# Two gathers a slot, one from each expert table, in place of one from the joined table

## The reference

```python
PEER_HEADS, PEER_TOPK, D_MODEL = 8, 16, 1024          # 128 experts a token
...
def peer_ffn(xn, w_query, sub_keys, expert_u, expert_v):   # tables: (16384, 1024) a layer
    ...
    idx = i1 * PEER_N_KEYS + i2
    g = jax.nn.softmax(cv, axis=-1)
    def block(args):
        xb, ib, gb = args
        hid = jax.nn.gelu(jnp.einsum('td,thkd->thk', xb, expert_u[ib]).astype(jnp.float32), approximate=False)
        return jnp.einsum('thk,thkd->td', (gb * hid).astype(xb.dtype), expert_v[ib])
...
for l in range(DEPTH):
    ...
    x = x + merged.astype(x.dtype) @ w_out[l]
    x = x + peer_ffn(rms_norm(x, norm2_w[l]), w_query[l], sub_keys[l], expert_u[l], expert_v[l])
```

## Time and profile before

| | |
|---|---|
| timed runs, median of 3 | 4050.73 us |
| span of the profiled execution | 5878.7 us |
| mean granted TensorE clock in it | 0.555 |
| PE, DVE, ACT, POOL busy | 97%, 49%, 28%, 22% |
| moved by DMA | 1444.45 MB, mean 246 GB/s |
| gathers | 1024 of 1 MB, 1237.6 us busy on POOL |
| the last stage | about 5000 to 5879 us |

### The profile page before, as it was taken

How to read it: one execution, slowest core, us unless ns; L and a number is a source line. 1 busy time by engine, 2 the same in 40 slices (tenths; PEclk the granted TensorE clock), 3 DMA queues, 4 the chain that set the end, 5 groups by cost and what they waited for, 6 DMA issues and landing times.

```text
span 5878.7 us, 40315 instructions
## 1 busy us (share of the span) xinstructions
PE 5726.4 (97%) x13374; PEld 2787.7 (47%) x13374; DVE 2887.4 (49%) x5745; ACT 1648.5 (28%) x4216; POOL 1285.3 (22%) x1094
## 2 busy tenths in 40 slices
PE   9999999999999998999999999899999999899999
PEld 5555555444444545444445545344445555222222
DVE  3321003665555455756555555756555554744443
ACT  3431101344422211244432211245422211222222
POOL 0000000222222221322222221322222221334343
PEclk6555555555555555555555555555555555555555
DMA  4222222767777775767777775777777775899997
GB/s 155 93 102 81 73 90 95 267 238 266 261 275 268 274 280 202 285 245 280 273 272 297 283 291 190 280 256 271 271 268 308 281 290 191 315 350 342 345 342 281
DMA packets 212948, 1444.45 MB, mean 246 GB/s; under 512 B 27256, under 2 KB 27256, under 8 KB 46340
## 3 DMA queue, kind: packets, MB, share of 16 engines
q0 software_dynamic: 164976, 1133.94, 52.0%
q1 hardware_dynamic: 47632, 307.80, 14.4%
q10 hardware_dynamic: 132, 0.12, 0.0%
HBM read 1439.31 MB, written 7.13 MB: 246 GB/s over the span
## 4 chain that ended last, share of the span: by engine, by line
PE 96%; DVE 2%; ACT 1%; issue 1%; DMA 0%; SPq 0%; ACTq 0%; DVEq 0%
PE banks L609 52%; PE sums L871 21%; PE banks L871 7%; PE banks L748 5%; PE banks L827 3%; PE banks L669 2%; PE banks L736 1%; PE banks L786 1%; PE banks L778 1%; PE banks L694 1%; PE banks L844 1%; DVE x L1479 1%; DVE rows L1470 0%; PE banks L637 0%; PE banks L700 0%
## 5 line engine op out<-in xcount | busy, mean ns | idle before, releaser
L609 PE MATMUL banks<-hT,ring 128*128 128x256 f32 x6656 | 2608.4, 583 | 4.7 <-DVE arena L1316 3.9
L609 PEld LDWEIGHTS banks<-hT,ring 128*128 128x128 f32 x6656 | 1507.5, 228 | 1151.7 <-issue 734.0
L576 POOL DMA_INDIRECT rows<-in_w_uv,idx x1024 | 1237.6, 1209 | 3600.3 <-PE sums L871 1981.3
L1470 DVE CUSTOM_DVE_ANT_0 rows<-rows,xn 128x1024 f32<-128x1024 f32 x1024 | 1241.6, 1220 | 530.8 <-DMA rows<-in_w_uv,idx 528.0
L871 PE MATMUL sums<-rows,diag 128*128 128x512 f32 x1612 | 1285.2, 970 | 70.0 <-ACT diag L1076 47.9
L1479 DVE SCALAR_TENSOR_TENSOR x<-rows,wgt,x 128x1024 f32<-128x1024 f32 x493 | 632.0, 1282 | 234.8 <-ACT wgt L1068 234.0
L871 PEld LDWEIGHTS sums<-rows,diag 128*128 128x128 f32 x1612 | 369.2, 232 | 791.7 <-issue 683.2
L1281 DVE SCALAR_TENSOR_TENSOR arena<-banks,pr,arena 128x254 f32<-128x254 f32 (+1 forms) x512 | 246.8, 482 | 354.6 <-ACT arena L965 340.9
L1063 ACT ACTIVATE gelu<-hid 128x2 f32<-128x2 f32 x512 | 102.9, 201 | 1100.7 <-DVE hid L1470 1099.3
L609 PE MATMUL banks<-yT,ring 128*128 128x256 f32 x1024 | 400.2, 582 | 0.0
L871 PE MATMUL banks<-rows,diag 128*128 128x512 f32 x512 | 393.7, 966 | 0.0
(11 more groups left out here) (205 smaller groups left out, 2955.8 us busy)
## 6 DMA issues: line engine op xcount, KB each, us to landing
ring<-in_w_ssd SPq DMA_DIRECT2D x96, 1024.0 KB, 5.4
ring<-in_w_att SPq DMA_DIRECT2D x64, 1024.0 KB, 6.1
ring<-in_w_mrg SPq DMA_DIRECT2D x52, 1024.0 KB, 8.4
arena<-a_rows POOLq DMA_DIRECT2D x32, 1024.0 KB, 7.6
ring<-in_w_qry SPq DMA_DIRECT2D x32, 1024.0 KB, 4.8
arena<-bias_tiles POOLq DMA_DIRECT2D x16, 1152.0 KB, 7.3
ring<-in_w_out SPq DMA_DIRECT2D x16, 1024.0 KB, 7.0
rows<-in_w_uv,idx POOLq DMA_INDIRECT x1024, 6.8
```

Source lines behind the costliest of these rows:

```text
L576: nc.gpsimd.indirect_dma_start(out=rows[n % NB][:, :], out_offset=None, in_=w_uv, in_offset=bass.IndirectOffsetOnAxis(ap=idx[:, t, s:s + 1 ...
L609: mm = pe.matmul(out, w[:, k * P:(k + 1) * P], rhs[:, k0 + k, :], start=start and k == 0, stop=stop and k == n - 1)
L1470: v.tensor_tensor_reduce(u, u, xn2[:, (n // SLOTS_T) % 3, :], 1.0, 0.0, ALU.mult, ALU.add, hid[:, k:k + 1]).then_inc(u_done, 1)
```

## The change

The joined table goes; `w_u` and `w_v` are two inputs. The eight buffers of 8 KB become sixteen of 4 KB: a ring of eight for u rows and a ring of eight for v rows, in the same room. Each slot has two gathers of 128 rows of 4 KB. On POOL, tick n issues the v gather of slot n + 4, when slot n - 4 is summed, and then the u gather of slot n + 7, when the dot product of slot n - 1 is done. The wait for `i_ok` goes with the u gather. DVE waits for the u row's landing before the dot product; PE and DVE wait for the v row's landing before the sum. Lines shift by up to 21 (L1470 becomes L1490, L871 becomes L891, L1479 becomes L1500; L576 stays).

```diff
--- before.py
+++ after.py
@@ -77,7 +77,8 @@
 
 NB = 8
 LAG = 3
-AHEAD = NB - LAG - 1
+AHEAD_V = NB - LAG - 1
+AHEAD_U = NB - 1
 DIAGS = 5
 
 BEHIND = 3.0
@@ -245,7 +246,7 @@
             tick(*todo.pop(0)[:2])
 
 
-def build(nc, x_prompt, x_sample, consts, biases, rel, par, w_ssd, w_att, w_mrg, w_out, w_qry, w_uv,
+def build(nc, x_prompt, x_sample, consts, biases, rel, par, w_ssd, w_att, w_mrg, w_out, w_qry, w_u, w_v,
           w_n2, w_final, y_prompt, y_sample):
     with ExitStack() as ctx:
         def sb(name, shape, dt=F32):
@@ -291,7 +292,9 @@
         gelu = sb("gelu", [P, SLOTS_P])
         wgt = sb("wgt", [P, SLOTS_P])
         diag = [sb(f"diag{n}", [P, P]) for n in range(DIAGS)]
-        rows = [sb(f"rows{n}", [P, 2 * D]) for n in range(NB)]
+        rows_all = sb("rows", [P, 2 * NB * D])
+        rows_u = [rows_all[:, n * D:(n + 1) * D] for n in range(NB)]
+        rows_v = [rows_all[:, (NB + n) * D:(NB + n + 1) * D] for n in range(NB)]
         late_keys = sb("late_keys", [P, 4 * SLOTS_T])
         iota16 = sb("iota16", [P, 16], BF16)
         ident = cst[:, C_ID:C_ID + P]
@@ -327,7 +330,7 @@
         junk = cut(D)
         n2b = cut(D)
         after_n = used[0]
-        first = rows[NB - 1]
+        first = rows_all[:, 2 * (NB - 1) * D:2 * NB * D]
         rel_w, hot_rel, mask_rel, row_rel = first[:, 3 * RW:3 * RW + NG * 8], first[:, 0:RW], first[:, RW:2 * RW], first[:, 2 * RW:3 * RW]
 
         used[0] = 0
@@ -447,7 +450,8 @@
         q_ev, q_s, q_sv = count("q_ev", 16), count("q_s", PH), count("q_sv", PH)
         k_v, i_ok, s_d, s_e, s_v2 = (sem(n) for n in ("k_v", "i_ok", "s_d", "s_e", "s_v2"))
         xn_ok = count("xn_ok", 2)
-        g_in = [sem(f"g_in{n}") for n in range(NB)]
+        u_in = [sem(f"u_in{n}") for n in range(NB)]
+        v_in = [sem(f"v_in{n}") for n in range(NB)]
         u_done, g_ge, g_w, d_ok, v_pe, v_dve = (sem(n) for n in ("u_done", "g_ge", "g_w", "d_ok", "v_pe", "v_dve"))
         x_add = count("x_add", 2)
         f_w, f_ss, f_v, f_sq, f_ok = (sem(n) for n in ("f_w", "f_ss", "f_v", "f_sq", "f_ok"))
@@ -564,27 +568,42 @@
                 pool.wait_ge(x_mid.sem, x_mid.at(m, 2))
                 pool.dma_start(n2b, w_n2[m // 2].partition_broadcast(P)).then_inc(n2_in.sem, 16)
 
-            def gather(n):
+            def gather(n, table, dst, landed):
 
                 p, k = n // SLOTS_P, n % SLOTS_P
                 t = 2 * (p % 2) + k // SLOTS_T
                 s = k % SLOTS_T
+                nc.gpsimd.indirect_dma_start(
+                    out=dst, out_offset=None, in_=table,
+                    in_offset=bass.IndirectOffsetOnAxis(ap=idx[:, t, s:s + 1], axis=0)).then_inc(landed, 16)
+
+            def gather_u(n):
+
+                p, k = n // SLOTS_P, n % SLOTS_P
                 if k == 0 or part_of(p, k) != part_of(p, k - 1):
                     pool.wait_ge(i_ok, part_of(p, k) + 1)
                 if n >= NB:
+                    pool.wait_ge(u_done, n - NB + 1)
+                gather(n, w_u, rows_u[n % NB], u_in[n % NB])
+
+            def gather_v(n):
+
+                if n >= NB:
                     summed(pool, n - NB)
-                nc.gpsimd.indirect_dma_start(
-                    out=rows[n % NB][:, :], out_offset=None, in_=w_uv,
-                    in_offset=bass.IndirectOffsetOnAxis(ap=idx[:, t, s:s + 1], axis=0)).then_inc(g_in[n % NB], 16)
+                gather(n, w_v, rows_v[n % NB], v_in[n % NB])
 
             def tick(p, k):
 
                 n = p * SLOTS_P + k
                 if n == 0:
-                    for first in range(AHEAD):
-                        gather(first)
-                if n + AHEAD < PASSES * SLOTS_P:
-                    gather(n + AHEAD)
+                    for first in range(AHEAD_U):
+                        gather_u(first)
+                        if first < AHEAD_V:
+                            gather_v(first)
+                if n + AHEAD_V < PASSES * SLOTS_P:
+                    gather_v(n + AHEAD_V)
+                if n + AHEAD_U < PASSES * SLOTS_P:
+                    gather_u(n + AHEAD_U)
 
             together(mixer, tick)
             pool.wait_ge(xn_ok.sem, xn_ok.at(PASSES, 0))
@@ -866,10 +885,11 @@
                     mine = [s for s in PE_SLOTS[p] if s // SLOTS_T == t]
                     if q == mine[0] and 2 * p + t and not (p == PASSES - 1 and t):
                         pe.wait_ge(x_add.sem, x_add.at(p, t))
+                    pe.wait_ge(v_in[n % NB], 16 * (n // NB + 1))
                     pe.wait_ge(d_ok, e + 1)
                     for h in range(2):
                         mm = pe.matmul(sum_banks(p, t)[:, h, :], diag[e % DIAGS][:, :],
-                                       rows[n % NB][:, D + 512 * h:D + 512 * h + 512], start=q == mine[0], stop=q == mine[-1])
+                                       rows_v[n % NB][:, 512 * h:512 * h + 512], start=q == mine[0], stop=q == mine[-1])
                     mm.then_inc(v_pe, 1)
 
             together(mixer, tick)
@@ -1465,18 +1485,19 @@
                 t = 2 * (p % 2) + k // SLOTS_T
                 if k % SLOTS_T == 0:
                     v.wait_ge(xn_ok.sem, xn_ok.at(p, k // SLOTS_T + 1))
-                v.wait_ge(g_in[n % NB], 16 * (n // NB + 1))
-                u = rows[n % NB][:, 0:D]
+                v.wait_ge(u_in[n % NB], 16 * (n // NB + 1))
+                u = rows_u[n % NB]
                 v.tensor_tensor_reduce(u, u, xn2[:, (n // SLOTS_T) % 3, :], 1.0, 0.0, ALU.mult, ALU.add, hid[:, k:k + 1]).then_inc(u_done, 1)
                 for q in sums_after(k):
                     if sum_on_pe(p, q):
                         continue
                     before = p * SLOTS_P + q
                     xo = x[:, 2 * (p % 2) + q // SLOTS_T, :]
+                    v.wait_ge(v_in[before % NB], 16 * (before // NB + 1))
                     v.wait_ge(g_w, before + 1)
                     if dve_sums(p, q) > 1:
                         v.wait_ge(v_dve, dve_sums(p, q) - 1)
-                    v.scalar_tensor_tensor(out=xo, in0=rows[before % NB][:, D:], scalar=wgt[:, q:q + 1], in1=xo,
+                    v.scalar_tensor_tensor(out=xo, in0=rows_v[before % NB], scalar=wgt[:, q:q + 1], in1=xo,
                                            op0=ALU.mult, op1=ALU.add).then_inc(v_dve, 1)
                 if k == SLOTS_T + LAG:
                     add_sums(p, 0)
@@ -1568,7 +1589,7 @@
         "rel": i["rel_bias"], "par": np.stack(par), "w_ssd": by_partition(np.stack(w_ssd)), "w_att": by_partition(np.stack(w_att)),
         "w_mrg": by_partition(np.stack(w_mrg)), "w_out": by_partition(i["w_out"].reshape(DEPTH, KD, P, D)),
         "w_qry": by_partition(np.stack(w_qry)),
-        "w_uv": np.concatenate([i["expert_u"], i["expert_v"]], axis=2).reshape(DEPTH * EXPERTS, 2 * D),
+        "w_u": i["expert_u"].reshape(DEPTH * EXPERTS, D), "w_v": i["expert_v"].reshape(DEPTH * EXPERTS, D),
         "w_n2": i["norm2_w"],
         "w_final": i["final_norm_w"],
     }
```

## The result

The changed kernel takes 4085.89 us (median of 4 runs, 4079.23 to 4090.88) against 4050.9 us before: a ratio of 1.0089, 95% interval 1.0074 to 1.0103, so 35 us slower. The forecast was 4183 us: the side is right, the size is nearly four times too large.

The account below looks back on a forecast made before the run. The prediction took DMA, at some 95% of what it can, to bound the timed runs. It summed 4050.73 + 105 (last stage) + 15 (beside the mixers) + 12 (turns of passes) = 4183 us, range 4040 to 4310 us.

Parts of the forecast that it names:

- POOL sets the last stage: Last stage: POOL's two gathers a slot, not DMA, set the pace, with 0.30 us gaps and POOL's busy share about doubled.
- The slot there goes from 2.61 to 3.02 us, +105 us: Last stage: each of 256 slots goes from DMA's 2.61 us to POOL's 3.02 us, +105 us (-13 to +282).
- the price of a gather, 1.209 us: On POOL: a 4 KB gather priced as the 8 KB one, 1.209 us plus 0.30 us gap, 3.02 us for two.
- My second way to it: Last stage: a dot product beginning at a chance place in POOL's beat delays the next gather 0.6 us, 3.1 us a slot.
- Beside the mixers +15 us: Three passes beside mixers: two gathers take 3.26 of a 3.57 us slot, mostly hidden, +5 us a pass, +15 us.
- the look-ahead that I put at 0: Whole kernel: issuing u rows seven slots ahead, v rows four as now, was priced at 0 us.
- The turn of a pass +12 us: Between passes: v gathers behind the wait for new expert numbers delay the last sums, 4 us three times, +12 us.
- The first: Rival, last stage: gathers rarely held, second gather hidden, DMA's 2.70 us sets the slot; 4086 us, chance 0.14.
- 23 us for packets: Last stage: 4 KB rows move 3.4% slower on DMA than 8 KB rows, costing 23 us unless POOL hides it.
- The second: Rival: earlier u rows save DVE waits beside the mixers and a deeper queue helps the last stage; 4013 us, chance 0.12.
- third: Rival: POOL binds beside the mixers too, from about 3.5 us for two gathers, +50 us a pass; 4318 us, chance 0.10.
- fourth: Rival: PE sets the timed last stage at 3.07 us, POOL stays hidden, only turns count; about 4055 us, chance 0.08.

Follow-up runs that it names:

- the one-input product: The changed kernel with its dot product replaced by a sum of the u row alone, one input from SBUF; 4044.65 us.

## Why the prediction was wrong in size

*POOL sets the last stage*: right. The gap before a gather is 0.30 us put down to issue, and POOL's busy share doubled (2336.6 us with 2048 gathers).

*The slot there goes from 2.61 to 3.02 us, +105 us*: this step failed. It went from 2.47 to 2.55 us in the middle and from 2.57 to 2.69 us over the whole stage (657 and 688 us for 256 slots), +31 us. Both ends of it were off. The smaller fault is before's: 2.61 us came from the median rate of the whole program, and the row at a full queue had 2.47 us (424 GB/s in the earlier trace rows; now 427). Taking it would have made the forecast still higher, by 36 us. The larger one is the price of a gather, 1.209 us. That mean was made of 0.94 us of work and a wait for DVE, and I took it to another beat of the engines as if it were work. It came from an execution in which PE set a 3.07 us slot and PE's sums released the gathers; in the faster execution of the same kernel the last stage has 0.99 us. My second way to it, a dot product at a chance place of the beat, gives 2.96 us and not 3.1 if the 0.48 us above is taken; it failed because in the changed kernel the places are not chance. There the product starts where it holds nearly nothing (2.55 us a slot). In the two kernels with fewer bytes, whose starts are spread, a slot takes 2.94 and 2.90 us: so the chance place was a fair price, but for another kernel.

*Beside the mixers +15 us*: -5 us. The number came near by luck, for two larger terms cancel in it. The second gather costs 55 us there, by POOL's second issue and perhaps by the 4 KB rows, which I had not priced in the passes at all: DMA, at 0.95 to 0.97 of its time before, is one of the things that those passes wait for, as the kernel with half the bytes shows (867 against 913 us). And the look-ahead that I put at 0 gave it back, 60 us with the rings.

*The turn of a pass +12 us*: the mechanism is there. On DVE, with the change:

```profile
1563.62 0.29 DVE L1220 TENSOR_TENSOR idx<-arena 128x128 uint32<-128x128 f32 x1
...
1575.36 1.33 DVE L1500 SCALAR_TENSOR_TENSOR x<-rows,wgt,x 128x1024 f32<-128x1024 f32 x1 [2.28 <-DMA rows<-in_w_v,idx]
1577.15 1.22 DVE L1480 TENSOR_TENSOR x<-x,sums 128x1024 f32<-128x1024 f32 x1 [0.46 <-DVE x L1500]
```

The last sum waits for its v row, and the closing add starts 13.5 us after the numbers; before, it was 7.1 us after them (1564.25 and 1571.32). That is 6.4 us more, where I had 2.1 to 5.3. Whether it costs the end anything isn't separated: it lies within the passes' -5 us, and the kernel with the wait at its old place, which also has the shorter look-ahead, lost 23 us there instead of gaining.

*Rivals.* The first gave 4086 us, and 4085.89 was measured, but by other steps: it took the slot for DMA's 2.70 us and had +12 us for the turns. Its core, that a gather is rarely held, is what happened in the last stage; beside the mixers the mean was 1152 to 1165 ns. Its 23 us for packets in the last stage were at most the 11 us that are left without holds. The second, earlier u rows, was real beside the mixers and was used up there. The third and fourth did not come. The 2.12 us that PE would need of a slot was too high, since it took the ratio of the spans for that of the clocks: with half the bytes PE, busy for 347 of 350 us, made 201 slots, 1.74 us each. Nothing in the sum hung on it.

The Trainium skill (SBUF — State Buffer, Who interferes with whom) says that an instruction of DVE with two SBUF inputs contends with GpSimd's reads, and that one with at most one SBUF input, outside the 2-port perf modes, does not. For the dot product the runs agree: the 722 gathers that start inside the one-input product take 0.94 us on average, the 654 that start inside the product of the changed kernel 1.39 us. The same section remarks that tensor_tensor did not stall DMA in its probe. These gathers don't fit that remark: the 24 of the changed kernel that start inside a plain TENSOR_TENSOR with two SBUF inputs (L1315) take 1.90 us.

## What to carry to other kernels

Split a mean duration into work and wait before it is taken to another stage or another clock: here the shortest and the median of the line showed the work (0.93 and 0.94 us), and the rest belonged to the phase between two engines. If one engine starts on what another one's transfer brings, look at where the starts fall in the timeline and don't average over it: the phase may have settled, and fewer bytes can then cost time, as they did here. And where DMA is as full as it was here (0.95 and more), price a second gather in every stage, and look-ahead too; the two can cancel, and only halves of the change show it.

## What was unexpected of the hardware

A gather of 128 rows takes POOL 0.94 to 0.95 us (median) and a gap of 0.30 us, whether its rows have 64 bytes, 2, 4 or 8 KB, so about 2.5 us is the least for two.

DMA sustained 427 GB/s with 8 KB rows at random places and 420 GB/s with 4 KB rows (shares 1.01 and 1.03).

The sum on DVE (L1500, two SBUF inputs as well) hardly holds gathers in the changed kernel: the 324 that start within it take 985 ns on average. With the one-input product the 300 that do take 1567 ns. So two SBUF inputs alone don't tell whether a gather is held, and why the sum holds in one company and not in the other stays open.
